# A hybrid decoder step on one core: feed-forward products taken from the undivided residual

## The reference

```
x = x + rmsnorm(cross_attention(...), norm_x_post)
h = rmsnorm(x, norm_ffn_pre)          # x * rsqrt(mean(x*x) + 1e-6) * g, per token
up = h @ w_up                          # 2048 -> 2 * 5632
c  = depthwise causal convolution of up over time (3 taps) + conv_b
y  = (gelu(c[gate]) * c[value]) @ w_down
x  = x + rmsnorm(y, norm_ffn_post)
def rmsnorm(x, g):  return x * rsqrt(mean(x * x, -1) + EPS) * g
```

## Time and profile before

| | us |
|---|---|
| median of 3 executions | 2735.86 |
| lowest, highest | 2730.3, 2737.19 |
| the profiled execution | 2728.69 |
| its span in the profile | 2727.0 |

### The profile page before, as it was taken

The page is one execution under the profiler, slowest core; times in us unless marked ns, Lnnn a source line. Parts: engine busy times, 40 slices in busy tenths (PEclk is TensorE's granted clock), DMA queues, the critical chain, the costliest instruction groups (busy, mean ns, idle before and its releaser), DMA issues. The chain is left out here.

```text
span 2727.0 us, 52522 instructions
## 1 busy us (share of the span) xinstructions
PE 2611.6 (96%) x20839; PEld 2495.9 (92%) x20839; DVE 1549.4 (57%) x1940; ACT 1225.0 (45%) x1534; POOL 193.3 (7%) x303
## 2 busy tenths in 40 slices
PE   6799999999999999999999998999899999999997
PEld 5778879899999999999999988898799999999997
DVE  4455554544555555654564547454766665666666
ACT  5344444432443443443343544334555555444553
POOL 0011121100011111100000000320000000000000
PEclk9899999999999999999999999999899999999998
DMA  5686786766888888885666755865366656666563
GB/s 148 180 275 194 228 278 195 240 183 166 234 231 229 220 237 236 220 224 162 178 172 180 233 138 153 278 208 167 97 185 182 168 169 196 182 182 185 162 178 115
DMA packets 856553, 530.80 MB, mean 195 GB/s; under 512 B 13169, under 2 KB 834345, under 8 KB 855647
## 3 DMA queue, kind: packets, MB, share of 16 engines
q1 hardware_dynamic: 822583, 440.07, 58.8%
q0 software_dynamic: 25728, 83.34, 9.0%
q10 hardware_dynamic: 8128, 5.76, 0.7%
HBM read 499.79 MB, written 33.29 MB: 195 GB/s over the span
## 5 line engine op out<-in xcount | busy, mean ns | idle before, releaser
L518 DVE TENSOR_TENSOR weights_lo<-weights_raw,weights_hi 128x2048 fp32r<-128x2048 f32 x407 | 932.3, 2291 | 769.9 <-ACT weights_hi L511 769.1
L542 PE MATMUL bank<-h_hi,weights_hi 128*128 128x264 f32 x4624 | 1333.3, 288 | 35.8 <-DVE weights_lo L518 15.7
L543 PE MATMUL bank<-h_lo,weights_hi 128*128 128x264 f32 x4624 | 1314.6, 284 | 0.0
L544 PE MATMUL bank<-h_hi,weights_lo 128*128 128x264 f32 x4624 | 1313.1, 284 | 0.0
L542 PEld LDWEIGHTS bank<-h_hi,weights_hi 128*128 128x128 f32 x4624 | 875.5, 189 | 57.3 <-issue 26.2
L543 PEld LDWEIGHTS bank<-h_lo,weights_hi 128*128 128x128 f32 x4624 | 876.2, 189 | 2.0 <-issue 1.9
L511 ACT ACTIVATE weights_hi<-weights_raw 128x2048 fp32r<-128x2048 f32 x407 | 776.9, 1910 | 214.8 <-PE bank L544 205.0
L544 PEld LDWEIGHTS bank<-h_hi,weights_lo 128*128 128x128 f32 x4624 | 871.3, 188 | 0.0
L542 PE MATMUL bank<-y_hi,weights_hi 128*128 128x264 f32 x1232 | 351.9, 286 | 7.3 <-DVE y_lo L2413 3.8
L544 PE MATMUL bank<-y_hi,weights_lo 128*128 128x264 f32 x1232 | 350.6, 285 | 0.0
L543 PE MATMUL bank<-y_lo,weights_hi 128*128 128x264 f32 x1232 | 349.0, 283 | 0.0
(11 more groups left out here) (374 smaller groups left out, 2169.3 us busy)
## 6 DMA issues: line engine op xcount, KB each, us to landing
weights_raw<-in_w_in SPq DMA_DIRECT2D x177, 1024.0 KB, 6.6
weights_raw<-in_w_up SPq DMA_DIRECT2D x88, 1024.0 KB, 5.9
weights_raw<-in_w_down SPq DMA_DIRECT2D x64, 704.0 KB, 4.7
gla_state_sample<-in_state_gla POOLq DMA_DIRECT2D x32, 512.0 KB, 6.2
out_gla_s<-gla_state_sample POOLq DMA_DIRECT2D x32, 512.0 KB, 6.9
weights_raw<-in_w_br_gla SPq DMA_DIRECT2D x16, 1024.0 KB, 5.9
weights_raw<-in_w_mix_out SPq DMA_DIRECT2D x16, 1024.0 KB, 5.9
weights_raw<-in_w_xkv SPq DMA_DIRECT2D x16, 1024.0 KB, 6.0
```

Source lines behind the costliest of these rows:

```text
L518: nc.vector.tensor_tensor(w_lo[:, r, :], raw[:, r, :], w_hi[:, r, :].bitcast(F32), ALU.subtract).then_inc(lo_ready, 1)
L542: nc.tensor.matmul(out, wh, xh, start=first and n == 0, stop=False)
L543: nc.tensor.matmul(out, wh, xl, start=False, stop=False)
L544: mm = nc.tensor.matmul(out, wl, xh, start=False, stop=last and n == len(blocks) - 1)
```

## The change

The feed-forward's h is no longer divided by the root mean square: h = x * g, and each up product is divided when its bank is emptied. In detail:

- `merged` takes the post gain already when ACT empties the attention's output; the residual update is a plain add, in eight groups of two tiles.
- ACT makes h_hi and the square of a tile directly from the new residual; DVE makes h_lo directly from it, before the next group's add.
- PE starts on up slots 0 and 1 together, block by block as h_lo comes (`up_block`); the sums of squares (`square_sum`) lie between these blocks, 32 columns wide, tile t in strip t % 4 of bank 7. Slot 2 follows ten blocks behind (LAG). Once eight of its blocks are done, the four strips are added by one more product with ones.
- The turns of the old rows go before the last slot of the attention's output; the weight split behind that slot goes to ACT behind the first root, and to DVE behind the fourth group.
- The first body of six up slots is written out, in both halves.
- DVE multiplies every up bank by 1/rms into a buffer of `squares` (this empties the bank), and ACT's convolution term and DVE's taps read that buffer. DVE's split of the weights comes right behind that multiplication, and is one slot later than before (slot j's in the work on slot j+1); the splits of the first two slots are kept where they were.

```diff
-                copy(merged[:, ds(n, 1), :], out[:, None, :])
+                nc.scalar.activation(merged[:, ds(n, 1), :], out[:, None, :], ACT.Copy, scale=scale)
...
-            norm(1, PC_FPRE)
+            act.wait_ge(*V_N[1].at("var"))
+            nc.scalar.activation(rstd[:, :], rstd[:, :], ACT.Sqrt).then_inc(A_N[1]("root"), 1)
+            split_hi(act, PH_XO_E, 1)
+            for c in range(8):
+                act.wait_ge(*V_N[1].at(f"x{c}"))
+                for t in (2 * c, 2 * c + 1):
+                    nc.scalar.activation(h_hi[:, t, :], xres[:, t, :], ACT.Copy, scale=param(PC_FPRE, t))\
+                        .then_inc(A_N[1](f"hi{t}"), 1)
+                for t in (2 * c, 2 * c + 1):
+                    if t >= 3:
+                        act.wait_ge(*P_N[1].at(f"s{t - 3}"))
+                    nc.scalar.activation(sqr[:, t % 3, :], xres[:, t, :], ACT.Square).then_inc(A_N[1](f"q{t}"), 1)
+            act.wait_ge(*V_N[1].at("var2"))
+            nc.scalar.activation(rstd[:, :], rstd[:, :], ACT.Sqrt).then_inc(A_N[1]("root2"), 1)
...
-                        act.wait_ge(*p.saved(j - 1, i))
+                        act.wait_ge(*V.at(f"u{j - 1}", i))
...
+                    act.wait_ge(*p.saved(j, i))
                     c = (cg, cv)[kind][:, q, :]
-                    nc.scalar.activation(c, bank[p.outs[j]][:, 0:T], ACT.Identity, scale=param(PC_CW + 176 + col, n),
+                    nc.scalar.activation(c, sqr[:, j % 3, :], ACT.Identity, scale=param(PC_CW + 176 + col, n),
...
+            def square_sum(t):
+                r = 32 * (t % 4)
+                pe.wait_ge(*A_N[1].at(f"q{t}"))
+                nc.tensor.matmul(bank[7][r:r + 32, 0:T], ones[:, 0:32], sqr[:, t % 3, :], start=t < 4, stop=t >= KB - 4)\
+                    .then_inc(P_N[1](f"s{t}"), 1)
...
+            LAG = 10
+            pe.wait_ge(*V_N[1].at("var"))
+            for n in range(KB):
+                pe.wait_ge(*V_N[1].at(f"lo{n}"))
+                for j in range(2):
+                    mm = up_block(j, n)
...
+                if n >= 2:
+                    square_sum(n - 2)
+                if n >= LAG:
+                    up_block(2, n - LAG)
+            square_sum(KB - 2)
+            square_sum(KB - 1)
+            for n in range(KB - LAG, KB):
+                if n == KB - LAG + 2:
+                    pe.wait_ge(*V_N[1].at("four"))
+                    nc.tensor.matmul(bank[7][:, 0:T], ones[:, :], acc[:, :], start=True, stop=True).then_inc(P_N[1]("all"), 1)
+                mm = up_block(2, n)
...
+            for c in range(8):
+                m, x = merged[:, 2 * c:2 * c + 2, :], xres[:, 2 * c:2 * c + 2, :]
+                nc.vector.tensor_tensor(m, m, rstd[:, None, :].to_broadcast([P, 2, T]), ALU.mult).then_inc(V1(f"yr{c}"), 1)
+                if c:
+                    low(c - 1)
+                dve.wait_ge(*V1.at(f"yr{c}"))
+                nc.vector.tensor_tensor(x, x, m, ALU.add).then_inc(V1(f"x{c}"), 1)
+                if c == 3:
+                    split_lo(dve, PH_XO_E, 1)
+            low(7)
...
+                    dve.wait_ge(projected, p.c(j, i) + 1)
+                    nc.vector.tensor_tensor(u, bank[p.outs[j]][:, 0:T], rstd[:, :], ALU.mult).then_inc(evac[p.outs[j]], 1)
+                    for low in lows:
+                        split_lo(dve, *low)
...
-                    split_lo(dve, p, j, i)
-                with dve.Fori(0, 7) as i:
...
+                with dve.Fori(1, 7) as i:
                     for j in range(6):
-                        conv(up, A_F[half], V_F[half], j, i, i * 3 + j // 2)
+                        conv(up, A_F[half], V_F[half], j, i, i * 3 + j // 2, [(up, j - 1, i) if j else (up, 5, i - 1)])
                 for j in range(2):
-                    conv(up_e, A_FE[half], V_FE[half], j, 0, 21)
+                    conv(up_e, A_FE[half], V_FE[half], j, 0, 21, [(up_e, 0, 0) if j else (up, 5, 6)])
+                split_lo(dve, up_e, 1)
```

More of the change, by code:

```diff
@@ L1426, in conv @@
                         copy(y_hi[:, ds(n, 1), :], cv[:, q:q + 1, :]).then_inc(S(f"hi{q}"), 1)
-                    split_hi(act, p, j, i)
-                with act.Fori(0, 7) as i:
+                    if not hi_first:
+                        split_hi(act, p, j, i)
+                for j in range(6):
+                    conv(up, A_F[half], V_F[half], j, 0, j // 2, half == 0 and j < 2)
+                with act.Fori(1, 7) as i:
                     for j in range(6):
@@ L1968, in _ @@
                     xo_slot(PH_XO, j, i)
-            for j in range(2):
-                xo_slot(PH_XO_E, j, 0)
-            norm(1, V_OUT["xo_end"].at("acc3"))
+            xo_slot(PH_XO_E, 0, 0)
             pe.wait_ge(hr_in, 16)
```

113 lines of the change are left out of this document (73 added, 40 removed).

## The result

The changed kernel takes 2740.49 us, median of 12 executions (2735.29 to 2742.43); the kernel before, on the same chip, 2734.75 (2730.3 to 2738.73). The two medians lie 5.7 us apart. The ratio on record, which is taken over all the executions and is not the quotient of the two medians, is 1.0018 with a 95% interval of 1.0009 to 1.0026: 4.9 us slower, inside the 0.3% that was called no change. Timed again beside other kernels it gave 1.0018 [1.0008, 1.0028]. The forecast was 2738.3, in 2728 to 2748, and +2.4 us.

A forecast was written before the change was run, and what follows sets the result against it. PE, busy 96% of the span, was taken to bound the kernel, with one gap at the feed-forward's norm. A kept lead of -1.0 us and +3.4 at the halves' ends gave +2.4: 2738.3 on the median 2735.86, range 2728 to 2748.

The forecast's parts named there:

- Head of the gap and first block: Between last attention product and up slot 0: head gains 1.3 us, PE's first up block at 1914.6, 17.6 us earlier.
- The clock: At the first up blocks: after 5.4 us idle PE runs at half clock until 1919.2, an estimated 0.66 us per block.
- Rival 2: Interleave of first up slots: clock stays at 1.2 GHz throughout, lead -8.1, sum +11.5 us, 2747.4; chance 0.10.
- Pairs: Tile pairs of slots 0 and 1: a loop of three engines sets 3.05 us per pair, 4.3 at pair 3.
- The price of a sum: Each 32-column sum between full-width blocks costs 0.63 us, ends 0.45 and 1.0.
- Slot 3: PE waits 3.0 us there for low weights queued behind the second root; it starts at 1950.6.
- Slots 5 and 6: Up slots behind slot 3: PE waits 0.4 and 0.6 us; from slot 7 the lead is 1.0 us.
- The stream: Up-slot loops: DVE's extra product fits, 10.5 us per two slots against 11.6 on PE; price 0.
- rival 3: Up-slot loops: DVE cannot hold two slots in 11.6 us; 2744 us and up; chance 0.05.
- The ends of the halves: Before each half's second down slot: y_lo 2.1 us later, PE waits 1.7 us, twice, 3.4 us.
- Rival 4: End of each half costs nothing, another order of arrival; sum -1.0 us, 2734.9; chance 0.08.
- Rival 1: Interleave runs freely, narrow sums 0.12 us, clock holds; lead 8.5, sum -5.1 us, 2730.8; chance 0.15.

The follow-up runs named there:

- six buffers: Changed kernel with each square in one of six buffers, so ACT's square t waits for sum t-6, not t-3; ratio to the kernel before 1.0004.
- full-width sums: Changed kernel with sums of squares 128 columns wide over all tiles, without the strips' copy and last sum; ratio to the kernel before 1.0001.
- sums in fours: Changed kernel with nine buffers for squares and the narrow sums grouped by four, one per column strip; ratio to the kernel before 0.9990.
- lows behind: Changed kernel with each low weight split at the halves' ends directly behind its slot's convolution, after the taps; ratio to the kernel before 1.0013.
- taps first: Changed kernel with slot 0's end split moved behind the first pair of convolutions, two splits behind one another; ratio to the kernel before 1.0025.
- fours and lows behind: Changed kernel with nine buffers and narrow sums grouped by four, plus low splits at the halves' ends behind the taps; ratio to before 0.9989.
- changed again: The changed kernel timed and profiled a second time, nothing altered; ratio to the kernel before 1.0018.

## Why the prediction was right

The forecast (+2.4 us, no change by its bound) came out at +4.9 by the ratio and +3.2 by distance, with the mechanism that it named: a lead from the earlier start, given back at slot 3 and at the halves' ends. Two sizes were off, one step had another limit than I named, and one cost took another form. Step by step:

- **Head of the gap and first block.** Forecast from the last attention product to the first block 8.2 us, measured 1922.05 - 1913.66 = 8.4.
- **The clock.** Half clock for 6 us from the first block and not 4.6. Rival 2 (half clock throughout the interleave) fell: 1.00 from 1930 to 1955. But one of my signs of being wrong, 0.50 beyond 1921, did come in part: behind slot 3 the products are 0.22 us apart again for 3 us (1958.85 to 1961.93).
- **Pairs.** 3.05 forecast, 2.98 measured, but for another reason. I took the loop hi, lo, blocks, sum, square for the limit and PE for 2.7 us of it; six buffers showed PE to be the limit, with 1.49 per tile. With full-width sums a pair takes 2.90 with a wait of 0.28 for h_lo in it, so a loop of about that length is there, and PE's work, with the dearer sum, had passed it. That the pair came out right is luck: two limits lie 0.1 us apart, and I had named the wrong one.
- **The price of a sum: mis-sized.** 0.63 forecast between 0.45 and 1.0, measured 0.77 = 0.45 + 0.09 in + 0.23 out, in 15 visits and not the 14 behind my 28 changes. The error of about 2 us hardly moved the forecast, since up to tile 9 I let the loop and not PE set the pace. I had taken the way out to cost what the way in does. The Trainium skill (TensorEngine Tiling (Array Packing), Key Properties) says "Changing tiling mode (not just tile) drains the TensorE"; the trace agrees, with about a third of a microsecond for both changes, less than the whole drain behind my 1.0. The same section has tiles work independently, and that too is what the group of four shows. The lower end of 0.12 per sum, from the earlier trace rows, is near what a group comes to (0.78 / 4 = 0.20) and far from a single one.
- **Slot 3.** Wait forecast 3.0, measured 2.68; lead there forecast 2.0, measured 47.7 - 44.4 - 1.4 = 1.9.
- **Slots 5 and 6: wrong in kind.** I forecast waits of 0.4 and 0.6; there are none. In their place the clock fell behind the wait at slot 3. From slot 3 to the first down product are 41 slots of 5.80, 237.8 us; the changed kernel takes 239.5, the kernels without the spell 238.6. So what I forecast as 1.0 is 0.8 where the clock holds (one wait of 0.3 shows there, at slot 6) and 1.7 where it doesn't. The lead at the first down product is 0.2 instead of 1.0: this is the 0.8 us by which the sum was short.
- **The stream.** Price 0 forecast and measured; rival 3 fell.
- **The ends of the halves.** 1.7 each forecast; the wait is 1.36, and the distances between the points give 1.7 and 1.7. The 0.3 more is the restart: the first product behind the wait takes 0.39 us, its weight load starts with it and not ahead of it (2202.99), and the next product starts 0.22 later. Rival 4 fell. By cause the step was incomplete: I put the whole on the product and the split ahead of the taps, and moving the splits back gave only 0.5.
- **Rival 1** (a free interleave, narrow sums at 0.12) did not occur in the changed kernel, and its price per sum is near what a group of four comes to. Its total of -5.1 is close to the -5.7 of sums in fours by distance (-2.7 by the ratio), but the clock fell there too, so the likeness is partly chance.

So where did the gain go? The first block does start 17.4 us earlier (27.3 us behind the last attention product before, 8.5 and the turns' 1.4 after). But from it to slot 3 PE took 20.4 us before and takes 35.9 now. In these, worked out from PE's rows: 48 blocks 17.4, 15 visits to narrow sums 11.6, half clock for 6 us about 2.8, the wait at slot 3 2.7, a wait for the tile behind slot 2's split 0.9, the strips' sum 0.5. Before, the 16 sums stood in a gap in which PE waited anyway; now they stand among products that PE could have been doing. 1.9 us of lead are left, the clock spell and DVE's queue take 1.7 of them, and the ends of the halves cost 3.4: 3.2 us in all.

## What to carry to other kernels

A row in which narrow products follow one another tells nothing of one that stands alone: price the change of tiling by itself, in and out, and group the narrow work. When a chain is moved behind a product, count how many products stand behind the last input of the chain; that the chain is off one path does not mean that something covers it at its new place. And compare profiles between fixed points near the change: here the distance between two of them repeated to 0.1 us in three profiles of one kernel and in two of the other, where whole executions scatter by 11. But look at the granted clock between the points as well: one profile of code that is the same up to the first down product came out 1.8 us shorter there, because the clock rose earlier and then held.

## What the runs showed of the hardware

- A change from full-width to 32-column products costs 0.09 us on the way in and 0.23 on the way out, and four narrow products on four strips take the time of one (0.78 against 0.77).
- **A clock that falls behind a wait of 2.7 us, but not always.** Behind the same wait of 2.68 us at slot 3 the granted clock read 0.87 and then 0.78 in the changed kernel, 0.66 in its second profile (1960 to 1965) and 0.77 with the lows behind, but 1.00 with the taps first, with six buffers, with sums in fours and with fours and lows behind. In the kernel with full-width sums it read 0.71 around a wait of 1.96. The Trainium skill (TensorE: Matmul & The Clock Gate, HAM oscillation) tells of waits between groups of products that throttle the clock; these rows agree in kind, with a shorter wait than those in its example. What decides whether it falls these rows don't say. It isn't the code alone: up to slot 3 changed, changed again, lows behind and taps first run the same, and the clock fell in the first three and not in the fourth.
- Filling a wait with products that nobody reads held the granted clock at 1.00 until 7.5 us behind the first up block (to 1926), where in the changed kernel it reads 0.50 from 4 us ahead of that block to 6 behind it, and gained nothing where another engine sets the pace behind it.
